# RWKV scan: each head's tokens kept on the half of the partitions that holds its channels, with 64 by 64 products on two quadrants of the array

## Chip, core and metric

The kernel runs on one core of a Trainium2 chip. The metric is the device time of one execution in microseconds (us). PE is the tensor engine (PEld its weight loads), DVE the vector engine, ACT the scalar engine, POOL GpSimd, SP the engine that issues most DMAs.

## What is computed

Two transformer blocks over 512 latent and 256 context tokens of width 1024. The change lies in the second layer of the first block, the RWKV mixer: 16 heads of 64 channels, a state S of 64 by 64 per head, in two directions (forward and backward), first over the context tokens (only the state is kept), then over the latent tokens with output.

```python
def step(s, inp):
    rt, wt, kt, vt, at, bt = inp
    sa = jnp.einsum('bhij,bhj->bhi', s, at)
    s = s * wt[:, :, None, :] + sa[..., None] * bt[:, :, None, :] + vt[..., None] * kt[:, :, None, :]
    y = jnp.einsum('bhij,bhj->bhi', s, rt) if with_out else None
    return s, y
```

The rest of the program (attention, an mLSTM, MLPs, a gated linear attention, experts) is the same before and after.

## The kernel before

The program is written by hand, engine by engine. Every engine runs its instructions in the order of the code, and waits on semaphores for what it needs. PSUM is one ring of eight banks: `K.bank(...)` takes the next one, and waits until whoever read the bank eight takes ago has freed it.

**Projections (`rw_in_*`).** r, v and k are products of the 768 tokens with 1024 by 1024 weights, each split into a rounded part and a rest, so three products each (L770). r and k are made with channels on the partitions (`columns`, 512 and 256 tokens wide), v with tokens on the partitions (`rows`, weights of 256 columns as the moving side, into `a.vR`).

**Scan (`rw_turns`, `rw_pe`, `rw_dve`, `rw_act`, `rw_pool`).** A step of 64 tokens is turned into matrix products. A *unit* is one direction d, one pair of heads m (128 channels: head 0 on partitions 0 to 63, head 1 on 64 to 127), and 256 tokens, that is four chunks of 64. There are 24 units per direction: for each of eight pairs a context unit (b = 0), then two latent ones (b = 1, 2). `rw_turns` lays them out as a pipeline. In iteration n, of twelve turns, both directions *solve* unit n (invert a 64 by 64 triangular matrix per chunk and head), *prepare* unit n+1 (elementwise work), and *stream* unit n-1 (the recurrence, three turns for each chunk). There are three kinds of iteration, which repeat eight times:

- A (n = 0, 3, ...): solves a context unit, streams the last latent unit of the pair before;
- B (n = 1, 4, ...): solves a latent unit, streams a context unit, and holds the norm of the keys of the next pair (`kk`) and the group norm of the outputs of the pair before (`end`);
- C (n = 2, 5, ...): solves a latent unit, streams a latent unit.

**Solve.** Turn 0 makes the gram products (L2355: a with b, and b with a and r); turn 1 the products with k (L2355 again) and four full 128 by 128 transposes of b and k (L2397, L2398), which put tokens on the partitions. Before the change the token chunk j decides on which half of the partitions a product lands, and head hd is in the free dimension, so the gram goes through all four 64 by 64 quadrants of the array. Turns 2 to 5 (squares and X add) and 6 to 9 (blocks of the inverse) are 64 by 64 products on the two diagonal quadrants (L2364, L2418). Between them ACT copies (L2742, L2746) and DVE adds (L2607, L2615, L2622).

**Prepare.** Turn 1 has the low-rank product of a unit (L2377, L2378: 64 rows, 128 columns, 256 tokens; "lora" below), turns 3 to 9 scans, exponentials and multiplications on DVE, ACT and POOL.

**Stream.** For each chunk, part 0 makes `rh` (L2446: a 128-row product with the state `zm`, held as a 128 by 128 matrix with two zero blocks; L2448: two 64 by 64), ACT copies it (L2755), part 1 makes `uu` (L2455), ACT copies it (L2761), part 2 makes `zz` (L2464, four 64 by 64) for the next state, and for latent units the output y (L2470: a 128 by 128 with the state; L2474: four 64 by 64). DVE makes the next state from `zz` (L2639, two instructions, one for each half), with POOL's scaled old state (L2842). At a given chunk the forward direction uses one half of the partitions for tokens, the backward one the other.

A float32 product that is not a transpose stands in the trace as two instructions, so counts there are twice those of the code. A transpose is one.

Of the kernel before, what the change touches and what calls it, by code (L numbers as in the profile page):

```python
# [529 lines left out]
def plan_layer1(K, w_at):  # L530
# [11 lines left out]
    a.vR = hpf[:, 0:6144].rearrange("p (x c) -> p x c", x=6)  # L542
# [21 lines left out]
    for d in range(2):  # L564
# [3 lines left out]
        s.sets = [(K.alloc(2, 4, 64), K.alloc(4, 2, 64), K.alloc(4, 64), K.alloc(2, 2, 128)),  # L568
# [3 lines left out]
                   bk[d].rearrange("p (a i c) -> p a i c", a=2, i=2))]  # L572
        s.RH, s.UU = K.alloc(128), [K.alloc(128) for _ in range(2)]
        z = K.Cf[:, 1600:1984] if d == 0 else K.alloc(384)
        s.zm, s.zg = [z[:, 0:128], z[:, 128:256]], z[:, 256:384]
# [9 lines left out]
    r.sq, r.kavh = K.alloc(768), K.Cf[:, 2024:2032]  # L585
    r.y = K.ring("y", ybufs)
# [1592 lines left out]
def rw_in_pe(K):  # L2179
# [12 lines left out]
    for g in range(12):  # L2192
        what = "rvk"[g // 4]
        lo = a.xx_lo if what == "k" else a.mix_lo
        ready = lambda k: K.at("rw lo", what, k)

        def x(k, x0, x1):
            return a.hi[:, k, x0:x1], lo[:, k, x0 + 1 + x0 // 512 * 2:x1 + 1 + x0 // 512 * 2]

        if what == "v":  # L2200
            through(w.rows(g, "rw v", g - 4, x, ready, wide=g == 4))
        else:
            through(w.columns(g, "rw " + what, 2 * (g % 4), x, BOTH, ready, wide=g % 4 == 0))


def rw_in_act(K):
# [12 lines left out]

    def rows(g):  # L2220
        n = 1 if g == 4 else 2
        for x in range(6 // n):
            s.wait_ge(K.at("rw v", g - 4, x))
            s.e.activation(a.vR[:, n * x:n * x + n, (g - 4) * 256:(g - 3) * 256],
                           K.ps.of("rw v", g - 4, x)[:, 0:n * 256].rearrange("p (x c) -> p x c", x=n), ACT.Copy).then_inc(
                *s.up(free("rw v", g - 4, x)))
# [26 lines left out]
    for g in range(4, 7):  # L2253
        rows(g)
# [3 lines left out]
    rows(7)  # L2258
# [3 lines left out]
    for g in range(8, 12):  # L2262
        columns(g, "rw k", a.kT)
        if g < 10:
            w.act(2 + g)

# [13 lines left out]
class Unit:  # L2280
# [23 lines left out]
    def chunk(self, sub):  # L2304

        it, j = sub // 2, sub % 2 ^ self.d
        return it, j, (*self.key, sub)
# [38 lines left out]
def rw_pe(K):  # L2346
    a, pe = K.a1, K.pe

    def gram(u, out, at, lhs, rhs):

        for it in range(2):
            for j in range(2):
                for hd, o in halves():
                    t = u.toks[it][j]
                    mm = pe.e.matmul(out[hd][half(j), it, at, :], lhs[o, t], rhs[o, :, t], start=True, stop=True)  # L2355
                    if it and j:
                        yield hd, mm

    def blocks(ps, o, lhs, rhs):

        for g in range(4):
            for j in range(2):
                h = half(j)
                mm = pe.e.matmul(ps[h, o + g * 64:o + g * 64 + 64], lhs[h, g, :], rhs[h, g, :], start=True, stop=True)  # L2364
        return mm

    for what, turn, u in rw_turns(K):
        if what == "kk" and turn == 2:
            pe.wait_ge(K.at("kk sq", u))
            for j, (x0, x1) in enumerate(BOTH):  # L2370
                ps = K.bank("norms", u, j)
                pe.e.matmul(ps[:, 0:x1 - x0], K.blk, K.rw.sq[:, x0:x1], start=True, stop=True).then_inc(
                    *pe.up(("norms", u, j)))
        if what == "prep" and turn == 0:
# [5 lines left out]
        if what == "solve":  # L2380
# [3 lines left out]
            if turn == 0:  # L2384
                pe.wait_ge(K.at("made", *u.key))
                out = [K.bank("gram", *u.key, hd)[:, 0:384].rearrange("p (i x c) -> p i x c", i=2, x=3) for hd in range(2)]
                for hd, mm in gram(u, out, slice(1, 2), u.aa, u.ops[:, 1:2, :]):
                    pass
                for hd, mm in gram(u, out, slice(0, 3, 2) if u.lat else slice(0, 1), u.bb, u.ops[:, to, :]):
                    mm.then_inc(*pe.up(("gram", *u.key, hd)))  # L2390
            if turn == 1:
                out = [K.bank("ka", *u.key, hd)[:, 0:256].rearrange("p (i x c) -> p i x c", i=2, x=2) for hd in range(2)]
                for hd, mm in gram(u, out, slice(0, 2 if u.lat else 1), u.ks, u.ops[:, to, :]):
                    mm.then_inc(*pe.up(("ka", *u.key, hd)))
                ps = K.bank("bk", *u.key)
                for it in range(2):
                    pe.e.transpose(ps[:, it * 128:it * 128 + 128], u.bb[:, u.tok[it]], K.ident)  # L2397
# [1635 lines left out]
```

## Time and profile before

| | us |
|---|---|
| median of 3 runs (lowest, highest) | 3886.99 (3884.51, 3895.28) |
| the profiled execution | 3884.07 |
| its span | 3882.3 |

| engine | busy us | share | instructions |
|---|---|---|---|
| PE | 3559.7 | 92% | 31848 |
| PEld | 2596.1 | 67% | 31848 |
| DVE | 1654.1 | 43% | 3457 |
| ACT | 1193.9 | 31% | 2457 |
| POOL | 400.9 | 10% | 608 |

The scan lies at about 1546 to 2445 us of the span. The table is an average over stages with different limits; what an edit is worth is read from its own stage. In a timeline row the first number is the start, the second the time from the first start to the last end of the merged instructions, the last "x" their count, and the bracket the idle time ahead with what ended it. The end of a matmul is later than the start of the next one that follows it at full rate, so rates come from differences between starts, or between ends.

### The profile page before, as it was taken

Reading aid. Unit: us, or ns where it says so; the run is one execution under the profiler, and the core shown is the slowest. Engines: PE = TensorE matmul, PEld = TensorE weight load, DVE = VectorE, ACT = ScalarE, POOL = GpSimd, SP = SyncE. Lnnn points to the kernel's source line nnn. Section 1 sums busy time; section 2 is a strip of 40 time slices with the busy share of each in tenths; the row PEclk is TensorE's granted clock in tenths of the full one; section 3 lists DMA queues with packets and bytes.
Section 4 is the critical chain, followed back from the end, with each engine's and each line's share of the span. In section 5 each row is a group of like instructions: output and inputs, shape, how many; then the busy total and the mean of one; then the engine's idle time right before and its main releaser. Section 6 shows DMA issues by size and latency. Waiting matters only on the chain.

```text
span 3882.3 us, 72541 instructions
## 1 busy us (share of the span) xinstructions
PE 3559.7 (92%) x31848; PEld 2596.1 (67%) x31848; DVE 1654.1 (43%) x3457; ACT 1193.9 (31%) x2457; POOL 400.9 (10%) x608
## 2 busy tenths in 40 slices
PE   7999998999999799799999999799998899698997
PEld 3565567788888498677877777478877677443332
DVE  1253345433333631666666665243343564311112
ACT  2242023412212322454545454232233332200001
POOL 0000122100001000222222222000000300000000
PEclk9999999999999899899999999699999899799998
DMA  5283043211111110000000000222221121489996
GB/s 212 96 338 128 28 163 120 87 65 66 66 66 66 40 66 5 5 4 4 4 4 4 5 4 3 114 88 87 95 79 63 44 92 75 170 366 427 427 428 265
DMA packets 34923, 433.83 MB, mean 112 GB/s; under 512 B 4992, under 2 KB 5600, under 8 KB 9136
## 3 DMA queue, kind: packets, MB, share of 16 engines
q1 hardware_dynamic: 29664, 413.44, 26.7%
q0 software_dynamic: 4944, 15.74, 1.3%
q8 instruction: 252, 4.13, 0.4%
q14 instruction: 63, 0.52, 0.0%
HBM read 423.92 MB, written 5.24 MB: 111 GB/s over the span
## 4 chain that ended last, share of the span: by engine, by line
PE 79%; DMA 9%; DVE 5%; ACT 5%; issue 1%; POOL 1%; SPq 0%; DVEq 0%; ACTq 0%; POOLq 0%
PE ps L770 16%; PE ps L1936 7%; PE ps L1937 7%; PE ps L1938 7%; PE ps L2364 7%; PE ps L711 4%; PE ps L3690 4%; DMA part<-in_wd 4%; DMA part<-in_wg 3%; PE ps L694 3%; PE ps L2446 2%; PE ps L2448 2%; PE ps L1016 2%; PE ps L2470 1%; ACT L71 1%; PE ps L2474 1%
## 5 line engine op out<-in xcount | busy, mean ns | idle before, releaser
L770 PE MATMUL ps<-part 128*128 128x512 f32 (+1 forms) x3312 | 624.0, 351 | 30.5 <-DVE part L1001 11.2
L770 PEld LDWEIGHTS ps<-part 128*128 128x128 f32 x3312 | 532.5, 193 | 122.6 <-DVE part L1001 12.4
L1936 PE MATMUL ps<-part 128*128 128x512 f32 (+1 forms) x1536 | 548.7, 357 | 18.0 <-DVE part L1983 11.4
L1937 PE MATMUL ps<-part 128*128 128x512 f32 (+1 forms) x1536 | 547.9, 357 | 0.0
L1938 PE MATMUL ps<-part 128*128 128x512 f32 (+1 forms) x1536 | 547.6, 357 | 0.0
L3690 PE MATMUL ps<-part 128*64 128x512 f32 x1536 | 377.3, 613 | 38.6 <-DMA part<-in_wd 16.4
L2364 PE MATMUL ps<-part 64*64 64x64 f32 x9984 | 360.9, 221 | 20.8 <-ACT part L2742 10.9
L1960 DVE TENSOR_TENSOR part<-part 128x1024 fp32r<-128x1024 f32 x128 | 158.6, 1239 | 493.6 <-ACT part L1949 493.6
L2364 PEld LDWEIGHTS ps<-part 64*64 64x64 f32 x9984 | 331.7, 135 | 49.7 <-ACT part L2742 17.5
L1936 PEld LDWEIGHTS ps<-part 128*128 128x128 f32 x1536 | 289.7, 189 | 67.8 <-DVE part L1983 12.6
L1937 PEld LDWEIGHTS ps<-part 128*128 128x128 f32 x1536 | 289.7, 189 | 46.4
L1938 PEld LDWEIGHTS ps<-part 128*128 128x128 f32 x1536 | 289.6, 189 | 46.3
L3690 PEld LDWEIGHTS ps<-part 128*64 128x64 f32 x1536 | 126.5, 140 | 270.5 <-issue 188.7
L1949 ACT ACTIVATE part<-part 128x1024 fp32r<-128x1024 f32 x128 | 135.6, 1060 | 485.8 <-PE ps L1938 485.3
L860 POOL TENSOR_TENSOR part<-part 128x512 f32<-128x512 f32 (+1 forms) x48 | 55.8, 1170 | 1765.8 <-ACT part L852 1212.7
L746 DVE TENSOR_TENSOR part<-part 128x2048 fp32r<-128x2048 f32 x40 | 91.4, 2290 | 236.0 <-ACT part L741 235.9
L711 PE MATMUL ps<-part 128*128 128x512 f32 x384 | 172.0, 604 | 2.8 <-ACT part L942 2.4
L711 PEld LDWEIGHTS ps<-part 128*128 128x128 f32 x384 | 73.5, 194 | 91.1 <-issue 88.5
L2639 DVE SCALAR_TENSOR_TENSOR part<-ps,part 64x64 f32<-64x64 f32 x320 | 90.2, 282 | 88.6 <-PE ps L2464 81.2
L694 PE MATMUL ps<-part 128*128 128x256 f32 (+1 forms) x384 | 126.4, 485 | 0.0
L3758 DVE TENSOR_TENSOR part<-part,ps 128x512 f32<-128x512 f32 x32 | 22.0, 688 | 240.1 <-PE ps L3664 113.5
L741 ACT ACTIVATE part<-part 128x2048 fp32r<-128x2048 f32 x44 | 83.8, 1910 | 94.4 <-PE ps L770 70.6
(414 smaller groups left out, 4920.7 us busy)
## 6 DMA issues: line engine op xcount, KB each, us to landing
part<-in_ada_w SPq DMA_DIRECT2D x36, 2048.0 KB, 9.3
part<-in_mlp_w SPq DMA_DIRECT2D x32, 2048.0 KB, 8.0
part<-in_wg SPq DMA_DIRECT2D x32, 2048.0 KB, 22.2
part<-in_wu SPq DMA_DIRECT2D x32, 2048.0 KB, 22.2
part<-in_wd SPq DMA_DIRECT2D x32, 2048.0 KB, 22.2
part<-in_b_in SPq DMA_DIRECT2D x8, 2048.0 KB, 7.9
part<-in_ab_w_in SPq DMA_DIRECT2D x7, 2048.0 KB, 8.7
part<-in_rkv SPq DMA_DIRECT2D x6, 2048.0 KB, 8.1
```

Source lines behind the costliest of these rows:

```text
L694: mm = pe.e.matmul(ps[:, 0:b - a], w[:, k, m:m + 128], h[:, k, a:b], start=k == 0, stop=k == kt - 1)
L711: mm = pe.e.matmul(ps[:, 0:n], h[:, k, o:o + 128], w[:, k, :], start=k == 0, stop=k == kt - 1)
L746: v.e.tensor_tensor(self.rest(g), self.tile(g), self.first(g), SUB).then_inc(*v.up((name, "split", g)))
L770: mm = pe.e.matmul(ps[:, j * n:j * n + n], lhs, rhs, start=k == ks[0] and i == 0, stop=k == ks[-1] and i == 2)
L1936: pe.e.matmul(ps, wh[:, k, :], hi[:, k, x0:x1], start=k == 0, stop=False)
L1937: pe.e.matmul(ps, wh[:, k, :], lo[:, k, x0:x1], start=False, stop=False)
L1938: mm = pe.e.matmul(ps, wl[:, k, :], hi[:, k, x0:x1], start=False, stop=k == 7)
L1949: s.e.activation(b.W[t % 2][0], src, ACT.Copy).then_inc(*s.up(self.key("rounded", t), self.key("split", t), *([("free", "w") + self.key("w ...
L1960: v.e.tensor_tensor(wl, src, wh, SUB).then_inc(*v.up(self.key("split", t), *([("free", "w") + self.key("w", p)] if c == 3 else [])))
L2364: mm = pe.e.matmul(ps[h, o + g * 64:o + g * 64 + 64], lhs[h, g, :], rhs[h, g, :], start=True, stop=True)
L2639: inst = v.e.scalar_tensor_tensor(out=z[o, o], in0=ps, scalar=gain[o], in1=s.zg[o, o], op0=MUL, op1=ADD)
L3690: mm = pe.e.matmul(ps[half(p), :], lhs(k, p), K.panel(8, 512, w, g, c, p)[:, k, :], start=k == 0, stop=k == 7)
```

## The change

- v is projected with channels on the partitions, like r and k (`a.vT`), and turned for each pair of heads in 64 by 64 blocks against the identity (a new helper `turned`, in B at turn 4, two banks), which ACT copies to `r.V` at turn 5 (two instructions). The transposes back at the end (L2494) are gone.
- A head's tokens now lie on the half that its channels lie on. Every product of solve and stream is 64 by 64, head 0 on one diagonal quadrant, head 1 on the other.
- The state is two 64 by 64 blocks above each other (128 partitions, 64 columns), without zero blocks. So the 128-row product in `rh` becomes two 64 by 64, and the 128 by 128 one in y also; DVE makes the next state in one instruction, and POOL scales half the columns.
- The four transposes of b and k become sixteen 64 by 64 products with the identity.
- The gram of turn 0 is only a with b both ways, in one bank. The products with k move from turn 1 to turn 10, that of b with r and the turned b and k to turn 11. Their masks and copies move along (DVE turns 10 and 11, ACT turn 11), and take one instruction where there were two.

```diff
-    def gram(u, out, at, lhs, rhs):
+    def gram(u, out, lhs, rhs):
         for it in range(2):
             for j in range(2):
                 for hd, o in halves():
                     t = u.toks[it][j]
-                    mm = pe.e.matmul(out[hd][half(j), it, at, :], lhs[o, t], rhs[o, :, t], start=True, stop=True)
+                    mm = pe.e.matmul(out[o, 2 * it + j], lhs[o, t], rhs[o, :, t], start=True, stop=True)
...
+    def turned(ps, o, blocks_of):
+
+        for i, block in enumerate(blocks_of):
+            for hd, h in halves():
+                mm = pe.e.matmul(ps[h, o + i * 64:o + i * 64 + 64], block[h, :], K.ident[h, h], start=True, stop=True)
         return mm
...
+        if what == "kk" and turn == 4:
+            for j, (x0, x1) in enumerate(BOTH):
+                ps = K.bank("v turned", u, j)
+                turned(ps, 0, [a.vT[:, u, x:x + 64] for x in range(x0, x1, 64)]).then_inc(*pe.up(("v turned", u, j)))
...
-                    pe.e.matmul(ps[h, 0:128], u.aa[:, cs], zm, start=True, stop=False, skip_group_check=True)
+                    for hd, o in halves():
+                        pe.e.matmul(ps[o, 0:64], u.aa[o, cs], zm[o, :], start=True, stop=False, skip_group_check=True)
...
-                    pe.e.matmul(ps[:, 0:64], zm, u.rr[:, cs], start=True, stop=False, skip_group_check=True)
-                    for k, w in enumerate((uu[h, :], vm)):
+                    sums = (zm, u.rr[:, cs]), (uu, u.Arb[:, g, :]), (vm, u.A[:, g, 1, :])
+                    for k, (w, A) in enumerate(sums):
                         for hd, o in halves():
-                            A = u.A[h, 2 * hd + it, 1, :] if k else u.Arb[h, 2 * hd + it, :]
-                            mm = pe.e.matmul(ps[o, 0:64], w[:, o], A, start=False, stop=k == 1, skip_group_check=True)
+                            mm = pe.e.matmul(ps[o, 0:64], w[o, :], A[o, :], start=k == 0, stop=k == 2, skip_group_check=True)
```

PE, turns 0 and 1 of an iteration that solves a latent unit, before: the two `rh` (L2446, L2448), then for each direction the products with k, four transposes and the low-rank pair.

```order
L2446 MATMUL ps<-part 64x128 [waits dve_wrote]
L2448 MATMUL ps<-part 64x64 x2
L2446 MATMUL ps<-part 64x128 [waits dve_wrote]
L2448 MATMUL ps<-part 64x64 x2
L2355 MATMUL ps<-part 64x128 x8
L2397 MATMUL ps<-part 128x128 [waits dve_wrote,act_wrote]
L2398 MATMUL ps<-part 128x128
L2397 MATMUL ps<-part 128x128
L2398 MATMUL ps<-part 128x128
L2377 MATMUL ps<-part 128x256 [waits landed_po0,landed_po1,dve_wrote,act_wrote]
L2378 MATMUL ps<-part 128x256
```

The same place after: `rh` is L2441 and L2443, the low-rank pair L2376 and L2377, `uu` L2449.

```order
L2441 MATMUL ps<-part 64x64 [waits dve_wrote]
L2441 MATMUL ps<-part 64x64
L2443 MATMUL ps<-part 64x64 x2
L2441 MATMUL ps<-part 64x64 [waits dve_wrote,act_wrote]
L2441 MATMUL ps<-part 64x64
L2443 MATMUL ps<-part 64x64 x2
L2376 MATMUL ps<-part 128x256
L2377 MATMUL ps<-part 128x256
L2376 MATMUL ps<-part 128x256 [waits act_wrote]
L2377 MATMUL ps<-part 128x256
L2449 MATMUL ps<-part 64x64 [waits act_wrote]
```

Nothing of 128 rows is left in `rh`, and the low-rank products of the two directions now stand side by side.

ACT, turns 4 to 6 of a B iteration, after: L2667 and L2669 are the key norm, L2724 the copies of squares, L2744 `uu`, L2758 the squares of y, L2675 the new copies of v, L2694 an exponential of the preparation.

```order
L71 ACT_TABLE_LOAD [waits dve_wrote]
L2667 ACTIVATE part<-part 128x768
L2669 ACTIVATE part<-part 128x768 [waits act_wrote]
L2724 ACTIVATE part<-ps 128x256 [waits pe_wrote] x2
L2744 ACTIVATE part<-ps 128x64 [waits pe_wrote] x2
L2758 ACTIVATE part<-part 128x512
L2675 ACTIVATE part<-ps 128x512
L2675 ACTIVATE part<-ps 128x256
L71 ACT_TABLE_LOAD [waits dve_wrote]
L2694 ACTIVATE part<-part 128x256
```

Before, the same stretch has no row between the squares of y (L2776) and the table load:

```order
L2742 ACTIVATE part<-ps 128x256 [waits pe_wrote] x2
L2761 ACTIVATE part<-ps 64x128 [waits pe_wrote] x2
L2776 ACTIVATE part<-part 128x512
L71 ACT_TABLE_LOAD [waits dve_wrote]
L2710 ACTIVATE part<-part 128x256
```

The two copies of v are the only thing that ACT has more there, and they are what frees the two banks that the turned v took.

## Rows read from the trace of the kernel before

**Rows 1.** Busy time by stretch: one A, one B, one C iteration.

```profile
core 0: us, PE busy (x) PEld busy (x) DVE busy (x) ACT busy (x) POOL busy (x), PEclk, DMA share, GB/s
1985.60:2018.30 32.70, 32.26 (x775) 27.66 (x775) 20.59 (x60) 15.96 (x50) 8.83 (x17) 1.00 0.01 4
2018.30:2058.90 40.60, 34.82 (x726) 27.14 (x728) 27.20 (x73) 23.58 (x54) 11.37 (x22) 0.96 0.02 6
2058.90:2093.10 34.20, 33.42 (x792) 28.36 (x784) 23.33 (x72) 14.79 (x47) 7.31 (x15) 1.00 0.01 4
```

**Rows 2.** The chain that ended last, a piece of an A iteration.

```profile
1996.17 2.80 PE ps L2364 x93
```

**Rows 3.** Timeline of PE in A: turn 9, both directions' part 0.

```profile
2006.64 0.63 PE L2364 MATMUL ps<-part 64*64 64x64 f32 x15
2007.20 0.43 PE L2446 MATMUL ps<-part 128*64 128x128 f32 x2
...
2007.93 0.43 PE L2446 MATMUL ps<-part 128*64 128x128 f32 x2
...
2008.52 0.22 PE L2448 MATMUL ps<-part 64*64 64x64 f32 x1
```

**Rows 4.** Timeline of PE in A: a latent part 2, both directions.

```profile
1994.16 0.28 PE L2364 MATMUL ps<-part 64*64 64x64 f32 x3
...
1994.59 0.43 PE L2470 MATMUL ps<-part 128*128 128x64 f32 x2
...
1995.94 0.23 PE L2474 MATMUL ps<-part 64*64 64x64 f32 x2
```

**Rows 5.** Timeline of PE: the gram of an A iteration, then of a B.

```profile
1985.70 1.10 PE L2355 MATMUL ps<-part 64*64 64x64 f32 x62
...
2018.40 1.51 PE L2355 MATMUL ps<-part 64*64 64x64 f32 x62
```

**Rows 6.** Timeline of PE in A, turn 1: transposes and lora of one direction.

```profile
1988.11 0.40 PE L2355 MATMUL ps<-part 64*64 64x64 f32 x7
...
1989.02 0.70 PE L2377 MATMUL ps<-part 64*128 64x256 f32 x2
...
1990.08 0.46 PE L2355 MATMUL ps<-part 64*64 64x64 f32 x16
```

**Rows 7.** Timeline of PE at the scan's start: both directions' lora together.

```profile
1558.73 1.23 PE L2377 MATMUL ps<-part 64*128 64x256 f32 x4
```

**Rows 8.** Timeline of PE in B: waits at turns 5 and 8.

```profile
2039.09 0.97 PE L2364 MATMUL ps<-part 64*64 64x64 f32 x26 [1.56 <-ACT part L2742]
...
2051.45 0.74 PE L2464 MATMUL ps<-part 64*64 64x64 f32 x16 [2.78 <-ACT part L2761]
```

**Rows 9.** Timeline of ACT in the same B.

```profile
2040.44 1.28 ACT L71 ACT_TABLE_LOAD   x1
...
2045.87 1.28 ACT L71 ACT_TABLE_LOAD   x1 [1.50 <-DVE part L2660]
```

**Rows 10.** Groups by line over the scan: DVE's state update, ACT's 512-wide copy.

```profile
L2639 DVE SCALAR_TENSOR_TENSOR part<-ps,part 64x64 f32<-64x64 f32 x306 | 86.2, 282 | 75.7 <-PE ps L2464 68.6 <-POOL part L2842 0.4
...
L2736 ACT ACTIVATE part<-ps 128x512 f32<-128x512 f32 x47 | 28.1, 599 | 5.5 <-PE ps L2398 4.0
```

**Rows 11.** Busy time of DVE, turns 3 to 9 of an A.

```profile
1995.70:2016.20 20.50, 15.89 (x46) 1.00 0.01 3
```

**Rows 12.** Busy time by stretch, just after the wait at turn 8.

```profile
2053.40:2056.60 3.20, 3.20 (x40) 2.57 (x37) 2.67 (x6) 0.84 (x2) 0.92 (x1) 0.50 0.00 0
```

**Rows 13.** Timeline of PE in the tail: two successive chunks.

```profile
2410.68 0.43 PE L2446 MATMUL ps<-part 128*64 128x128 f32 x2
...
2414.77 0.43 PE L2446 MATMUL ps<-part 128*64 128x128 f32 x2
```

**Rows 14.** Busy time of PE on L770: projection of r, then of v.

```profile
1333.10:1401.00 67.90, 67.81 (x384) 58.99 (x384) 1.00 0.09 31
1404.30:1474.10 69.80, 69.69 (x576) 69.67 (x576) 0.98 0.14 53
```

More of the change, by code:

```diff
@@ L2198, in x @@
             return a.hi[:, k, x0:x1], lo[:, k, x0 + 1 + x0 // 512 * 2:x1 + 1 + x0 // 512 * 2]
[L2200 to L2203, printed above, removed]
+        through(w.columns(g, "rw " + what, 2 * (g % 4), x, BOTH, ready, wide=g % 4 == 0))
 def rw_in_act(K):
@@ L2253, in rw_in_act @@
     for g in range(4, 7):
-        rows(g)
+        columns(g, "rw v", a.vT)
         w.act(2 + g)
@@ L2257, in rw_in_act @@
     first(a.xx, 0, "k")
-    rows(7)
+    columns(7, "rw v", a.vT)
     for k in range(1, 8):
@@ L2414, in rw_pe @@
                 pe.wait_ge(K.at("X", *u.key, 3))
-                for g in range(4):
-                    for j in range(2):
-                        h = half(j)
-                        mm = pe.e.matmul(ps[h, g * 64:g * 64 + 64], XX[h, 0, g, :], K.ident[h, h], start=True, stop=True)
-                mm.then_inc(*pe.up(("X turned", *u.key)))
+                turned(ps, 0, [XX[:, 0, g, :] for g in range(4)]).then_inc(*pe.up(("X turned", *u.key)))
             if turn in (6, 8):
@@ L2490, in rw_pe @@
                 pe.e.matmul(ps, K.blk, k0, start=True, stop=True).then_inc(*pe.up(("coef", m)))
-            if turn == 5:
-                ps = K.bank("v turned", m)
-                for x in range(4):
-                    mm = pe.e.transpose(ps[:, x * 128:x * 128 + 128], a.vR[:, x, m * 128:m * 128 + 128], K.ident)
-                mm.then_inc(*pe.up(("v turned", m)))
 def rw_dve(K):
@@ L2692, in rw_act @@
                 s.e.activation(r.sq, r.sq, ACT.Exp, scale=-0.5, bias=float(7 * np.log(2.0))).then_inc(*s.up(("kk rstd", m)))
+            if turn == 5:
+                if m >= 2:
+                    s.wait_ge(*[K.at("streamed", d, 3 * m - 4) for d in range(2)])
+                for j, (x0, x1) in enumerate(BOTH):
+                    s.wait_ge(K.at("v turned", m, j))
+                    s.e.activation(r.V[m % 2].rearrange("p x c -> p (x c)")[:, x0:x1], K.ps.of("v turned", m, j)[:, 0:x1 - x0],
+                                   ACT.Copy).then_inc(*s.up(("v rows", m), free("v turned", m, j)))
         if what == "prep":
@@ L2726, in rw_act @@
                     s.wait_ge(K.at(("PX", 2), u.d, u.n - 1))
[L2727 to L2732 removed]
+                s.wait_ge(K.at("gram", *u.key), K.at("masked", *u.key))
+                src = K.ps.of("gram", *u.key).rearrange("p (g x c) -> p g x c", g=4, x=2)
+                s.e.activation(t.Pf, src[:, :, 1, :], ACT.Copy).then_inc(*s.up(("Pf", *u.key), free("gram", *u.key)))
+            if turn == 11:
                 s.wait_ge(K.at("bk", *u.key))
```

171 lines of the change are left out of this document (72 added, 99 removed).

## The prediction, as put on record

> **What bounds the kernel now.** I read the busy time by stretch first [rows 1]. In all three kinds of iteration PE is the fullest engine: 32.26 of 32.7 us in A, 33.42 of 34.2 in C, at full clock, with DVE at 63 to 68% and ACT at 43 to 49%. In B it is different: PE 34.82 of 40.6, ACT 23.58, and two waits of PE of 1.56 and 2.78 us on ACT [rows 8]. So A and C are worth what PE is spared, as long as DVE keeps up, and B is worth what the chain through ACT is spared. A group of three takes 107.5 us, eight groups 860 us.
>
> Then the rate of small products. A stretch of L2364 has 93 instructions in 2.80 us, 0.030 each [rows 2]: two per 0.06 us, one on each diagonal quadrant. The gram, which goes through all four, has 62 in 1.10 us [rows 5], with 0.22 of that the last one's own length 0.0144 each: twice the rate. And a change of shape costs: two `rh` last from the end of L2364 (2006.64 + 0.63) to the end of the last L2448 (2008.52 + 0.22), 1.47 us for twelve instructions [rows 3].
>
> **The change, part by part.** Times are for both directions; all float32 products count as two instructions.
>
> *Part 0 (`rh`).* Eight products of one shape, 16 x 0.030 = 0.48, for 1.47: -0.99. A has four, C four, B three (the first context chunk has no state).
>
> *Part 2.* For a latent chunk 1.73 us from 1994.16 + 0.28 to 1995.94 + 0.23 [rows 4]. After, twenty products, 40 x 0.030 = 1.20: -0.53. The last chunk of a pair has no `zz`: about 1.45 before (1.73 less eight instructions), 24 x 0.030 = 0.72 after: -0.7. For a context chunk the two directions today can use four quadrants; 16 instructions cost 0.23 to 0.48 before and 0.48 after; I take +0.15 each, +0.6 in B.
>
> *Part 1* stays at eight instructions on two quadrants: nothing.
>
> *Gram.* It leaves four quadrants for two. A: 64 instructions, 0.92 to 1.92: +1.0. B and C: today 1.51 less 0.22, 1.3 us, in which half of the instructions are 128 columns wide; after 64 narrow ones, 1.92: +0.6.
>
> *Products with k.* A: 32 narrow ones, 0.46 to 0.96: +0.5. B and C: wide ones; from the B gram, (1.3 - 0.47) / 32 = 0.026 each on four quadrants, so 0.83 to 1.66: +0.83. *b with r* is new by itself in B and C: 32 x 0.030 = +0.96.
>
> *Transposes and lora.* For one direction from the last start of L2355 (1988.11 + 0.40 - 0.22) to its next at 1990.08 [rows 6], less one slot 1.75 us, so 3.5 for two. After, the turned blocks are 64 x 0.030 = 1.92 us. The two lora products now stand together. At the scan's start they already do, and four instructions take 1.23 us at half clock [rows 7], where two alone take 0.70 at full clock [rows 6]: they run side by side. So 1.06 (1989.02 to 1990.08) plus 0.2 for the change of shape, 1.26, and together 3.2: -0.3. If they ran one after the other, +0.7.
>
> *v.* B gets 48 x 0.030 = 1.44 us of turned v and loses four transposes with their changes of shape, at most 0.73 (1988.29 to 1989.02 in rows 6): +0.75. ACT gets a copy of 512 columns, 0.60 [rows 10], and one of 256, about 0.4.
>
> PE alone: A +1.0 +0.5 -0.3 -4.0 -1.6 -0.7 = -5.1. C +0.6 +0.83 +0.96 -0.3 -4.0 -2.1 = -4.0. B +0.6 +0.83 +0.96 -0.3 -3.0 +0.6 +0.75 = +0.4.
>
> *What comes through.* In A and C the cover is DVE. In turns 3 to 9 of A it is busy 15.89 of 20.5 us [rows 11]. The state update goes from four instructions of 0.282 [rows 10] to two for each chunk, -1.1 in these turns, so 14.8. PE's share of these turns goes from 20.5 to about 16.5 (three `rh`, two parts 2). DVE is then 90% full there and hands its results to PE in a chain, and I add 0.4 us of waits to A and 0.3 to C: -4.7 and -3.7. The moved products lie in turns 10 and 11, ahead of `uu` and `zz`, where they cover the copies of `rh` and `uu` on ACT.
>
> In B turns 0 to 3 lose 3.3 us on PE (gram +0.6, k -0.83, transposes and lora 3.5 to 1.26, one `rh` -1.0, `zz` +0.15), so ACT's chain of table loads and exponentials [rows 9] starts that much earlier. It gets 1.0 us of copies of v, which stand ahead of its second table load. They also free the two banks of the turned v. Six more banks are taken in turn 4, so the ring of eight comes round to the first of these two at the first X add of turn 5: **PE waits there for the copies**, some 2.9 us instead of 1.56. The wait at turn 8 is set by the same chain and is released 2.1 us earlier than today. Behind it PE has more to do: +1.66 +0.96 +1.92 -1.0 -0.7 +0.3, less 0.5 us of a wait that is now covered, +2.7. B comes out at +0.6.
>
> The clock belongs in this. After the wait at turn 8 the granted clock is 0.50 for 3.2 us (1.2 GHz) [rows 12], which costs 1.6 us in each B; it was 1.00 before. That stays in my sum. The trace has the slow clock behind a gap of 2.78 us, and the new wait at turn 5 is of that size. The Trainium skill (TensorE: Matmul & The Clock Gate, Why this matters for your kernels) advises against long idle gaps between bursts of matmuls, since idling brings the slow clock back; the trace agrees at turn 8, and the same thing at turn 5 is the second rival below.
>
> *Sum.* Seven A with a stream, 7 x -4.7 = -32.9; the first, with nothing to stream, +1.2; eight C, -29.6; eight B, +4.8. In the tail a chunk takes 4.1 us [rows 13], where PE, ACT and DVE take turns; PE is spared 1.5 us a chunk, four chunks, -6. The projection of v as columns costs what r costs, 67.9 for 69.8 [rows 14]: -1.9. At the scan's start ACT's copies add about 1. Together -63. From the profiled execution's 3884.1 that is 3821; the median of the runs lies 2.9 above that execution, so the forecast is 3824.
>
> **Rivals.**
>
> *DVE, and the chains through it, take half of what A and C gain.* Turns 3 to 9 shrink by 2 us instead of 4. For it: 90% of a chained engine; POOL's large multiplications slow DVE beside them. Against it: today these chains let PE wait under 1 us an iteration. Fifteen times +2: 3854.
>
> *A second spell of slow clock in B.* The wait at turn 5 grows to the size of the one at turn 8, and 1.7 us are lost behind it in seven B: 3836.
>
> *The lora products do not overlap at full clock.* +1.0 in 23 iterations: 3847.
>
> *Better.* The waits of A and C (0.4 and 0.8 us by rows 1) vanish with DVE's shorter updates, and B gains from its earlier chain: -27, 3797.
>
> *Slower: two quadrants for four, with nothing gained for it.* The added work (gram, k, b with r: 1.5 + 2.4 + 2.4, v 0.75, context 0.6, less 0.9 of lora) is 6.8 us in a group, the spared 15.3 (11 x 0.99, 7 x 0.53, 0.7). If what is spared is filled by waits, the kernel gets slower once less than 44% of it comes through; with none, 8 x 6.8 = +54 on today's 3887, 3941. That needs DVE to grow in turns 3 to 9 instead of shrinking, or a wait of 4 us in every A and C.
>
> *The two halves of a product share a bank, and exclude each other.* Every new product would then cost 0.060 an instruction instead of 0.030; some 1200 instructions in a group, +36 us, eight times: 4112. Against it: L2364 already writes both halves of one bank, at 0.030 [rows 2]. The Trainium skill (TensorEngine Tiling (Array Packing), Gotcha 1: PSUM Pressure) says that different row tiles cannot access the same PSUM bank at the same time; the trace of this kernel does not agree where the halves of the partitions differ.
>
> **How the numbers follow.** Forecast as summed 0.42; DVE takes half 0.18; slow clock 0.15; lora 0.07; better 0.12; slower 0.04; bank 0.02. The range from 3790 to 3858 takes in all but the last two and some spread around the others. A measurement of this kernel tells about 0.3%, 12 us, from no change. Faster by more than that holds all but 0.07; I split the rest into 0.03 within and 0.04 slower.
>
> **What would show it.** Part 0 of both directions in 0.5 us and part 2 in 1.2; the gram of A in 1.9; A near 28 us, C near 30.5, B near 41; DVE busy over 85% in turns 3 to 9; in B a wait of nearly 3 us before the X add of turn 5, released by ACT's copy of v, and the wait at turn 8 still there; L770 of v at 68 us. I am wrong if A and C keep more than 31 and 33 us with PE waiting for DVE, or if B grows by more than 3 us.

## The result, and the profile of the changed kernel

The changed kernel takes 3775.9 us (median of four runs, 3767.3 to 3785.3), the kernel before, timed beside it, 3889.8 (four runs, 3884.5 to 3895.3): a ratio of 0.971, 95% interval 0.968 to 0.974. That is 114 us less, where the forecast had 65; the time lies 14 us below the lower end of the range. Of the runs below, one execution of the split state update took 5785.6 us at a granted clock of 0.55 and is left out of its median.

The profiled execution is the slowest of the four, 3785.3 us. It comes to the stages ahead of the projections about 10 us later than the one of before, though nothing is changed there, so that the pair of traces differs by 99 us only. Its page:

```profile
span 3783.5 us, 77347 instructions
PE 3472.2 (92%) x34472; PEld 2594.7 (69%) x34472; DVE 1595.7 (42%) x3149; ACT 1152.0 (30%) x2426; POOL 387.6 (10%) x608
```

The three kinds of iteration, from gram to gram, answer [rows 1]; the fourth stretch, PE's turns 3 to 9 of A, answers [rows 11], and the fifth, behind the wait at turn 8 of B, [rows 12]:

```profile
core 0: us, PE busy (x) PEld busy (x) DVE busy (x) ACT busy (x) POOL busy (x), PEclk, DMA share, GB/s
1952.43:1978.93 26.50, 26.35 (x862) 25.70 (x860) 18.67 (x50) 13.38 (x47) 8.52 (x17) 1.00 0.02 5
1978.93:2019.07 40.14, 34.31 (x864) 29.45 (x862) 26.11 (x63) 22.41 (x56) 10.94 (x22) 0.96 0.03 7
2019.07:2047.78 28.71, 28.56 (x910) 27.91 (x908) 19.20 (x54) 13.22 (x46) 6.29 (x15) 1.00 0.02 4
1959.25:1975.20 15.95, 15.80 (x534) 15.58 (x532) 13.45 (x39) 7.24 (x28) 6.77 (x14) 1.00 0.02 5
2011.20:2014.40 3.20, 3.20 (x61) 3.16 (x62) 1.98 (x5) 1.04 (x3) 0.10 (x1) 0.60 0.00 0
```

A went from 32.7 to 26.5 us, C from 34.2 to 28.7, B from 40.6 to 40.1. In A and C, PE is now idle for 0.15 us. DVE's busy time in A fell by 1.9 us, ACT's by 2.6. PE's timeline over the start of an A (here line 2345 is the gram, 2441 and 2443 are `rh`, 2376 and 2377 lora, 2449 `uu`) answers [rows 3, 5, 6]:

```profile
1952.43 2.03 PE L2345 MATMUL ps<-part 64*64 64x64 f32 x64
1954.30 0.28 PE L2441 MATMUL ps<-part 64*64 64x64 f32 x4
1954.42 0.28 PE L2443 MATMUL ps<-part 64*64 64x64 f32 x4
1954.53 0.28 PE L2441 MATMUL ps<-part 64*64 64x64 f32 x4
1954.65 0.28 PE L2443 MATMUL ps<-part 64*64 64x64 f32 x4
1954.86 0.71 PE L2376 MATMUL ps<-part 64*128 64x256 f32 x4
1955.40 0.60 PE L2377 MATMUL ps<-part 64*128 64x256 f32 x4
1955.93 0.45 PE L2449 MATMUL ps<-part 64*64 64x64 f32 x8
```

The gram takes 1.87 us from start to start, part 0 of both directions 0.56 (0.47 where narrow products follow, at 1962.05 to 1962.52), and both lora 1.07 together, x4 and x4 where [rows 6] has x2 and x2 for one direction.

**Where the time went, term by term.** I charged each PE instruction of one group (A, B and C, gram to gram) with the time from its start to the start of the next; what is left of a gap behind the instruction's own length is a wait. So a change of shape is charged to somebody. In us a group:

| | before | after | difference | forecast |
|---|---|---|---|---|
| `rh` and `uu` | 19.31 | 9.37 | -9.9 | -10.9 |
| `zz` and `y` | 14.72 | 10.98 | -3.7 | -3.8 |
| gram, products with k, b with r | 7.60 | 11.90 | +4.3 | +6.3 |
| lora, transposes, turned blocks | 13.39 | 13.08 | -0.3 | -0.15 |
| L2364, now L2352 | 40.92 | 38.81 | -2.1 | 0 |
| norms and sums of the end (slow clock in one) | 4.67 | 5.08 | +0.4 | 0 |
| waits | 6.95 | 6.13 | -0.8 | +0.9 |
| group | 107.5 | 95.35 | -12.2 | -7.7 |

Four and a half us a group are 36 us in eight; the first and the last iterations, which are not quite like this group, bring that to 40 (from the first gram to the tail 96.5 us were saved, where the forecast had 56.5). The rest of what was missed, 9 us, is in the tail.

### The profile page after: what moved, and what is told of

Read it like the earlier page. It is cut to its first block, busy times and chain, and to the rows that moved or that the text cites. A ratio compares the mean times of both kernels' runs of the same rounds, so it can differ in the third digit from the quotient of the medians.

```text
span 3783.5 us, 77347 instructions
## 1 busy us (share of the span) xinstructions
PE 3472.2 (92%) x34472; PEld 2594.7 (69%) x34472; DVE 1595.7 (42%) x3149; ACT 1152.0 (30%) x2426; POOL 387.6 (10%) x608
## 4 chain that ended last, share of the span: by engine, by line
PE 78%; DMA 9%; DVE 6%; ACT 5%; issue 1%; POOL 1%; SPq 0%; DVEq 0%; ACTq 0%; POOLq 0%
PE ps L770 16%; PE ps L1936 8%; PE ps L1938 8%; PE ps L1937 8%; PE ps L2352 7%; PE ps L3672 5%; PE ps L711 4%; DMA part<-in_wd 4%; DMA part<-in_wg 3%; PE ps L694 3%; PE ps L2345 3%; PE ps L1016 2%; PE ps L2359 2%; PE ps L2467 1%; ACT L71 1%; PE ps L2458 1%
## 5 line engine op out<-in xcount | busy, mean ns | idle before, releaser
L770 PE MATMUL ps<-part 128*128 128x512 f32 (+1 forms) x3120 | 627.1, 363 | 30.7 <-DVE part L1001 11.0
L770 PEld LDWEIGHTS ps<-part 128*128 128x128 f32 x3120 | 525.7, 194 | 132.5 <-DVE part L1001 12.2
L2352 PE MATMUL ps<-part 64*64 64x64 f32 x9984 | 343.7, 220 | 20.7 <-ACT part L2675 11.9
L2352 PEld LDWEIGHTS ps<-part 64*64 64x64 f32 x9984 | 318.2, 136 | 48.8 <-ACT part L2675 12.8
L2345 PE MATMUL ps<-part 64*64 64x64 f32 (+1 forms) x2816 | 110.2, 230 | 11.2 <-DVE part L2552 11.2
L741 ACT ACTIVATE part<-part 128x2048 fp32r<-128x2048 f32 x44 | 83.7, 1910 | 95.1 <-PE ps L770 71.7
```

The lines of the kernel that those rows point to most:

```text
L770: mm = pe.e.matmul(ps[:, j * n:j * n + n], lhs, rhs, start=k == ks[0] and i == 0, stop=k == ks[-1] and i == 2)
L2345: mm = pe.e.matmul(out[o, 2 * it + j], lhs[o, t], rhs[o, :, t], start=True, stop=True)
```

## The experiments

Runs of different kernels are compared through their ratios to before, whose intervals are 0.13% to 0.2% to either side (0.3% for the changed kernel); the lengths of iterations in the traces are finer. Here they run from one lora product to the next (the start of turn 1), so they differ a little from those above. A and C are the usual values, B is the mean of six.

| | C | A | B | group | median us | ratio to before |
|---|---|---|---|---|---|---|
| before | 33.2 | 32.25 | 42.2 | 107.7 | 3889.8 | 1 |
| changed | 28.7 | 26.3 | 40.1 | 95.1 | 3775.9 | 0.971 |
| e1_wide | 32.8 | 30.3 | 43.7 | 106.8 | 3865.9 | 0.9935 |
| e2_narrow | 29.65 | 27.2 | 40.1 | 97.0 | 3794.8 | 0.975 |
| e3_copies | 28.8 | 26.3 | 41.0 | 96.1 | 3778.8 | 0.971 |
| e4_state | 29.8 | 26.9 | 41.4 | 98.1 | 3797.1 | 0.977 |
| e5_early | 29.8 | 29.1 | 40.8 | 99.6 | 3812.6 | 0.980 |
| e6_late_v | 31.1 | 26.3 | 39.8 | 97.2 | 3788.5 | 0.973 |
| e7_fill | 28.7 | 26.3 | 38.8 | 93.8 | 3770.1 | 0.969 |
| e9_apart | 30.0 | 27.6 | 40.8 | 98.4 | 3805.3 | 0.979 |
| e10_order | 28.7 | 26.3 | 37.6 | 92.6 | 3757.4 | 0.967 |
| e11_orders | 28.7 | 26.3 | 42.2 | 97.2 | 3790.3 | 0.975 |
| e12_best | 30.1 | 26.3 | 39.4 | 95.7 | 3778.5 | 0.973 |

**A wide product back in part 0.**

```diff
                     pe.wait_ge(K.at("zm", *c))
+                pe.e.matmul(ps[0:64, 128:256], u.aa[:, cs], K.ident, start=True, stop=True)
```

> The changed kernel with one product of 128 rows by 128 columns more at the head of every part 0, into columns of the bank that nobody reads: the shape change of before is back, with all else as changed. Theory (PE's own time sets A and C, and what the change bought there is shapes that no longer change): before, part 0 of one direction took 1.47 / 2 = 0.735 us, of which four narrow instructions at 0.030 are 0.12, so the wide pair with its changes of shape costs 0.6; eight of these in an iteration, 4.9 us, 24 iterations, 117, less what B's waits take up: +95 to +125 us on the changed kernel's 3776, which eats all of its gain. Rival (PE has room, and the gain came from ACT's and DVE's smaller tiles): less than +50. Tail: the granted clock of the last chunks goes back to 0.50 if the wide products are what it goes with.

Measured: +90 us, A +4.1, C +4.1, B +3.6. Divided by eight, a wide product among narrow ones costs 0.51 us, a little under the 0.6 expected, and so the total is just under the range expected. PE's timeline of two part 0 in this run (line 2440 is the added product):

```profile
1995.40 2.97 PE L2352 MATMUL ps<-part 64*64 64x64 f32 x96
1998.30 0.43 PE L2440 MATMUL ps<-part 128*64 128x128 f32 x2
1998.66 0.33 PE L2443 MATMUL ps<-part 64*64 64x64 f32 x4
1998.83 0.28 PE L2445 MATMUL ps<-part 64*64 64x64 f32 x4
1999.04 0.43 PE L2440 MATMUL ps<-part 128*64 128x128 f32 x2
```

From the wide one's start to the next start are 0.36 us, for two instructions. And 2443 and 2445 hold PE for 0.38 us, where without the wide ones they take 0.23: the change is paid on both sides. So the shapes are the main thing that the change bought; the run keeps the narrow products that took the wide one's place, 0.12 us each time, so it gives back somewhat more than part 0 had gained. The tail's clock stayed at 1.00: the wide products alone are not what its 0.50 goes with.

**The control: two narrow products instead.**

```diff
+                for hd, o in halves():
+                    pe.e.matmul(ps[o, 128:192], u.aa[o, cs], K.ident[o, o], start=True, stop=True)
```

> The control: the changed kernel with a 64 by 64 product on each diagonal quadrant more at the head of every part 0 (four instructions where the run with a wide product has two). No change of shape. Theory: four instructions at 0.029 are 0.12, eight times an iteration 0.94, all of it in A and C, less than half in B: +15 to +22 us. Rival (PE has room): under +5. If it costs as much as the wide one, the cost is not the shape but another link in the chain of a chunk.

Measured: +19 us, A and C +0.94 each, just the four instructions eight times. B stayed at 40.1. Twice as many instructions as the wide product at a quarter of its price: it is the shape, and A and C have no room for PE work.

**ACT's copies in two halves.**

```diff
+                for o in (slice(0, 32), slice(32, 64)):
+                    s.e.activation(t.RH[:, o], K.ps.of("rh", *c)[:, o], ACT.Copy)...   (and UU alike)
```

> The changed kernel with each of ACT's copies of rh and uu made as two copies of half the columns: about +0.2 us in the chain for each copy, four times what they got shorter by (0.27 to 0.225). Theory (A and C bound by PE): A and C get under 0.3 us more each, B, which waits for ACT, 1 to 1.5: +10 to +18 us in all. Rival (the waits that went, 0.3 in A and in C, went because of the shorter copies, and the chain of a chunk is close to setting the end): waits of 0.2 us at most of the eight chunks of A and C, +1 us or more each, +25 us or more.

Measured: +3 us, less than the +10 to +18 expected; A and C grow by under 0.1 in most of their iterations, B by 0.9. The rival falls. That ACT's copies got shorter did not take the waits of A and C away.

**DVE's state update in two halves.**

```diff
-                    inst = v.e.scalar_tensor_tensor(out=z, in0=ps, scalar=gain, in1=s.zg, op0=MUL, op1=ADD)
+                    for hd, o in halves():
+                        inst = v.e.scalar_tensor_tensor(out=z[o], in0=ps[o], scalar=gain[o], in1=s.zg[o], ...)
```

> The changed kernel with DVE's state update again as two instructions of 64 partitions, as before: +0.28 us on DVE for each chunk and direction. DVE is busy 13.45 of 15.95 us in turns 3 to 9 of A. Theory (PE sets A and C, DVE has room): under +0.2 us an iteration, +0 to +6 us. Rival (what I had not counted is that DVE's shorter updates took the waits of A and C away): the waits of 0.3 us come back and more, +0.5 us or more in A and C, +8 to +20 us.

Measured: +21 us (median of three runs; +24 by the ratios), C +1.1, A +0.6, B +1.3. Here the rival held, at the upper end of its range or above it. Six of this run's seven A take 26.9 us and have a wait of PE ahead of the second `rh` of turn 6 (first row) and one of 0.12. The second row is DVE at that place:

```profile
1874.58 0.33 PE L2441 MATMUL ps<-part 64*64 64x64 f32 x4 [0.25 <-ACT part L2742]
1873.21 1.22 DVE L2616 SCALAR_TENSOR_TENSOR part<-ps,part 64x64 f32<-64x64 f32 x4
...
1980.31 0.33 PE L2441 MATMUL ps<-part 64*64 64x64 f32 x4 [0.18 <-DVE part L2616]
```

Line 2616 is the state update, four instructions for the two directions, and the last ends at 1874.43, 0.15 us before PE goes on. (The copy that the first row names ends at 1874.59, after `rh` has started, so it was not what PE waited for.) In the seventh A, of 27.5 us, the profile names the update itself (last row). PE stands at `rh` until the state is there. One instruction of 128 partitions costs DVE what one of 64 cost, in the group over the scan:

```profile
L2615 DVE SCALAR_TENSOR_TENSOR part<-ps,part 128x64 f32<-128x64 f32 x160 | 40.5, 278 | 63.8 <-PE ps L2458 63.5
```

0.278 us for 0.282 twice [rows 10]. So of the 114 us some 21 to 24 rest on DVE's half of the change, and it is what keeps the waits away that I had put into the sum. A and C have 13 of them; of B's 1.3 a part is that the clock was slow for longer in three of its six B (42.3 us each, where two others took 41.1).

**The moved products back in turn 1.**

```diff
-            if turn == 10:
+            if turn == 1:          (k; and 11 to 1 for b with r and the turned blocks; on DVE and ACT alike)
```

> The changed kernel with the products with k, b with r and the turned b and k back in turn 1, where before had them; PE's products are the same ones. Theory (where they stand matters): in A and C they cover ACT's copies of rh and uu in turns 10 and 11, 0.3 to 0.6 us an iteration; in B they come ahead of ACT's chain and no longer behind it: +1 to +2 us. In all +12 to +30 us. Rival (PE is full in A and C wherever they stand, and B's chain has room): within 5 us of the changed kernel.

Measured: +37 us, A +2.8, C +1.1, B +0.7. The theory's total is passed, but not by its mechanism. By the same charging as above, lora goes from 3.28 us a group to 6.35, which is 3.1 of this group's 4.5 us: the moved products again stand between the two directions' lora. `uu` adds 0.9, for the copies are no longer covered. B did not get what was expected there.

**Lora apart.**

```diff
+            if u.d:
+                for hd, o in halves():
+                    pe.e.matmul(ps[o, 0:64], K.ident[o, o], K.ident[o, o], start=True, stop=True)
             pe.e.matmul(ps[:, 0:256], u.wm[u.rows, 0, :], a.wh[u.rows, u.lo:u.hi], start=True, stop=True)
```

> The changed kernel with one 64 by 64 product on each diagonal quadrant (four instructions, result overwritten) between the lora products of the two directions, which stand next to each other there. With the products moved back to turn 1 lora cost 6.35 us a group instead of 3.28. Theory (the two directions' lora run side by side, each on its half of the rows, only when they stand together, and that is what the moved products bought): +1.0 us for lora and 0.1 for the four instructions in each of 24 iterations, +22 to +28 us. Rival (it was the place of the moved products themselves): +3 us.

Measured: +29 us, C and A +1.3, B +0.7. PE's timeline with the four narrow instructions (line 2378) between:

```profile
1988.56 0.70 PE L2379 MATMUL ps<-part 64*128 64x256 f32 x2
1989.10 0.59 PE L2380 MATMUL ps<-part 64*128 64x256 f32 x2
1989.62 0.33 PE L2378 MATMUL ps<-part 64*64 64x64 f32 x4
1989.88 0.70 PE L2379 MATMUL ps<-part 64*128 64x256 f32 x2
1990.41 0.59 PE L2380 MATMUL ps<-part 64*128 64x256 f32 x2
```

Each direction takes 1.06 us again, one after the other, against 1.07 for both above. Four instructions between them undo the overlap. This settles the move: most of what it is worth is that lora stands together. The four are of another shape than lora; that instructions of the same shape between them would do the same was not tried.

**The turned v out of B.**

```diff
-        if what == "kk" and turn == 4:
+        if what == "v" and turn == 6:      (in the next iteration; ACT's copies in its turn 7)
```

> The changed kernel with the turned v and ACT's copies of it in the iteration after B (turns 6 and 7) instead of turns 4 and 5 of B. Theory (the 1.77 us wait at turn 5 of B is made by these copies): the wait goes, and B gets 1.4 us shorter by the products besides, less what the wait at turn 8 grows by; the other iteration gets 1.4 us longer, PE being full there. Net -0.5 to -1.5 us a group, -4 to -12 us. Rival (the chain of ACT's table loads sets B, and the wait at turn 8 takes over what the one at turn 5 gives): B shorter by no more than the products, 0 to +5 us.

Measured: +13 us, outside both ranges. B shrinks by 0.3 only, the other iteration grows by 2.4, of which 0.8 is a wait for this copy. In B the wait at turn 5 is still there, with another releaser, and the one at turn 8 a little longer:

```profile
1995.91 1.15 PE L2354 MATMUL ps<-part 64*64 64x64 f32 x32 [1.66 <-ACT part L2728]
...
2007.45 1.12 PE L2460 MATMUL ps<-part 64*64 64x64 f32 x16 [2.98 <-ACT part L2748]
```

L2728 is ACT's copy of the squares. In the changed kernel that wait names the copy of v (below), but taking it out gives 0.1 us: behind ACT's table load all its copies are late alike.

**Work in the gap at turn 8.**

```diff
+                if sub == 2 and u.b == 0 and u.d == 0:
+                    for i in range(16):
+                        for hd, o in halves():
+                            pe.e.matmul(ps[o, 256:320], u.aa[o, cs], K.ident[o, o], start=True, stop=True)
                 pe.wait_ge(K.at("uu in", *c), K.at("BK", *u.key))
```

> The changed kernel with 64 narrow instructions, 1.87 us, whose result nobody reads, ahead of the wait of 2.66 us at turn 8 of B. Theory (the granted clock of 0.60 in the 3.2 us behind that wait is due to the gap): the clock stays at 1.00 there and the wait is 0.8 us: 1.0 to 1.3 us less in each B, -8 to -10 us. Rival (the clock falls with something else, or the products delay what comes behind): 0 to +5 us.

The waits of B in the changed kernel, then what this run has at the same two places, then two stretches of this run, around the second wait and behind it:

```profile
1997.95 1.15 PE L2352 MATMUL ps<-part 64*64 64x64 f32 x32 [1.77 <-ACT part L2675]
...
2009.16 0.68 PE L2458 MATMUL ps<-part 64*64 64x64 f32 x16 [2.66 <-ACT part L2744]
```

```profile
1985.18 1.15 PE L2352 MATMUL ps<-part 64*64 64x64 f32 x32 [1.77 <-ACT part L2680]
...
1996.39 0.68 PE L2463 MATMUL ps<-part 64*64 64x64 f32 x16 [0.79 <-ACT part L2749]
```

```profile
1994.90:1998.40 3.50, 2.71 (x53) 1.75 (x51) 2.70 (x6) 1.55 (x6) 2.46 (x4) 1.00 0.02 5
1998.40:2001.00 2.60, 2.60 (x72) 2.60 (x70) 2.41 (x6) 1.05 (x3) 0.13 (x1) 1.00 0.03 6
```

The granted clock stays at 1.00, where it was 0.60, and every B is 38.8 us, 1.5 less than most in the changed kernel (40.4). By the runs -6 us, a little under what was expected, which alone the intervals do not tell from nothing. Work that nobody needs made the kernel no slower.

The gap does not bring the slow clock each time. In the changed kernel itself five B have the 2.66 us and the slow clock; the last two have as long a wait (2.66 and 2.60) and keep 1.00, and the first of these takes 38.8 us:

```profile
2199.86 0.68 PE L2458 MATMUL ps<-part 64*64 64x64 f32 x16 [2.66 <-ACT part L2744]
...
2201.90:2205.10 3.20, 3.20 (x90) 3.20 (x86) 2.83 (x7) 1.09 (x4) 0.10 (x1) 1.00 0.01 3
```

In the control with two narrow products, where that wait is 2.59 us, three of six B had the slow clock, in this run none of six.

**Work in the gaps of before's tail.**

```diff
                 ps = K.bank("uu", *c)
+                if u.n == UNITS - 1:
+                    for hd, o in halves():
+                        for i in range(2):
+                            pe.e.matmul(ps[o, 256:320], u.aa[o, cs], K.ident[o, o], start=True, stop=True)
                 pe.wait_ge(K.at("rh in", *c), K.at("X", *u.key, 5))
```

> The kernel before, with eight narrow instructions more (0.23 us, their result read by nobody) ahead of each wait for the copy of rh in the last iteration alone, for both directions. There its granted clock is 0.50 from 2415 to the end of the scan, a chunk takes 6.3 us, and the changed kernel has 1.00 and 2.6 us a chunk. Theory (short gaps bring the slow clock): the clock stays at 1.00 in the last chunks, -6 to -12 us on before. Rival (it is not the gaps): the clock falls as before, +1 to +3 us.

The tail by stretch, first the kernel before, then the changed one, then this run:

```profile
2411.00:2416.40 5.40, 5.11 (x66) 3.73 (x64) 1.13 (x4) 1.83 (x8) 0.99 (x3) 0.88 0.00 0
2416.40:2422.70 6.30, 5.95 (x58) 4.40 (x58) 1.13 (x4) 1.53 (x6) 0.80 (x2) 0.50 0.00 0
2422.70:2429.00 6.30, 5.95 (x57) 4.40 (x56) 1.13 (x4) 1.54 (x6) 0.00 (x0) 0.50 0.01 3
```

```profile
2325.00:2327.60 2.60, 2.60 (x72) 2.21 (x70) 0.57 (x3) 1.34 (x6) 0.58 (x2) 1.00 0.02 6
```

```profile
2416.00:2420.00 4.00, 3.93 (x72) 3.11 (x71) 0.91 (x4) 1.32 (x6) 0.49 (x3) 1.00 0.00 0
2420.00:2424.00 4.00, 4.00 (x73) 3.25 (x73) 1.14 (x4) 1.53 (x6) 0.73 (x2) 1.00 0.01 4
```

Measured: 3884.1 for 3893.3 beside it, ratio 0.998, interval 0.996 to 0.999, -9 us. Sixty-four added instructions bring the full clock back to the last chunks. Before, that clock fell with PE busy 5.11 of 5.4 us. From the first `rh` of the tail to the start of the last product of the scan before took 31.4 us, in this run 24.4, in the changed kernel 16.5. So of the -14.9 about 7 is this clock, a little over 6 the shorter chunks that the forecast had, and 1.5 the last products, where the transposes of v are gone. Each of these is one profiled execution; the ten of this run give -9 us with an interval of -4 to -14.

**ACT's order in turn 7 of B.** The turns list yields, for ACT alone and in this turn of B, the solve and the stream ahead of the preparation.

```diff
-    for what, turn, u in rw_turns(K):
+    for what, turn, u in rw_turns(K, (7,)):
```

> The changed kernel with ACT's order changed in turn 7 of B alone: its copies of uu come ahead of the four exponentials of the next unit and their table load, not behind them. The copies take 0.34 us; behind them PE waits 2.66 us at turn 8, and then has the slow clock. Theory (that wait is the place of two copies in ACT's queue, not the load of ACT): the wait falls under 0.5 us and the clock stays at 1.00: 2.5 to 3.5 us less in each B, -18 to -26 us. Rival (ACT's whole chain sets B, so that the wait turns up later, at the gram or at turn 9): 0 to -6 us.

Measured: 3757.4 us (3754.5 to 3759.5), ratio 0.967, interval 0.965 to 0.968. Every B is 37.6 us, 2.8 less than most in the changed kernel. The wait of 2.66 at turn 8 is gone; of what it held back, 1.04 shows up two steps later, released by DVE, with the clock at 1.00. This is at the lower end of what the theory expected. It is the fastest version here, 132 us under before (3757.4 for 3889.8) and 18 under the changed kernel.

```profile
1990.49 0.68 PE L2368 MATMUL ps<-part 64*64 64x64 f32 x16 [0.16 <-DVE part L2619]
...
1994.58 0.68 PE L2368 MATMUL ps<-part 64*64 64x64 f32 x16 [1.04 <-DVE part L2612]
```

**The same in turns 4 and 5.**

```diff
+    for what, turn, u in rw_turns(K, (4, 5, 7)):
```

> As the run with ACT's order changed in turn 7, and in turns 4 and 5 of B too: the copies of the solve and of the stream come ahead of the logarithm, the exponential and their table load, and ahead of the copies of v. Theory (the wait of 1.77 us at turn 5, too, is the place of a copy in the queue): 1.0 to 1.7 us less in each B than with turn 7 alone, -26 to -38 us on the changed kernel. Rival (the later logarithm makes kk late, and the next unit's operands with it): between the changed kernel and the run with turn 7 alone.

Measured: 3790.3, 33 us worse than turn 7 alone and 14 above the changed kernel: neither the theory nor the rival had it so slow. ACT now waits 1.97 us for the squares of turn 4, and only then come the table load, the logarithm and the exponential, and the copies of v (L2691) behind them; PE waits for those at turn 5:

```profile
1994.38 0.38 ACT L2740 ACTIVATE part<-ps 128x256 f32<-128x256 f32 x1 [1.97 <-PE ps L2368]
...
1999.38 0.85 ACT L2691 ACTIVATE part<-ps 128x512 f32<-128x512 f32 x2
```

```profile
2000.01 1.98 PE L2368 MATMUL ps<-part 64*64 64x64 f32 x32 [4.51 <-ACT part L2691]
```

**Turns 4 and 7, with v out of B.**

```diff
+    for what, turn, u in rw_turns(K, (4, 7)):
...
-        if what == "kk" and turn == 4:
+        if what == "v":                     (turn 10 of the iteration after B)
```

> A version meant to be faster. From the run with turn 7's order (3757), two more edits: the turned v and ACT's copies of it in turn 10 of the iteration before the one with k's products in A, out of B (in turns 6 and 7 of that iteration they cost 2.4 us, of which 0.8 is a wait for the copy), and in turn 4 of B ACT's copies of the solve come ahead of the logarithm and its table load. Theory (with the v copies gone, the wait at turn 5 is the place of a copy in ACT's queue behind the table load): B loses 1.4 us of products and up to 1.7 of the wait, the other iteration gains 1.4 to 1.6: -1.0 to -1.7 us a group, 3744 to 3750, 0.964 of before. Rival (the later logarithm sets B, as in the run where all the orders changed): 3757 or more.

Measured: 3778.5 (five runs), 21 us worse than turn 7 alone. The rival held. The logarithm that now starts later makes DVE's `kk` late, and that multiplication (L2525, on DVE) stands ahead of the X addition (L2606) that PE waits for:

```profile
1996.76 0.96 DVE L2525 TENSOR_TENSOR part<-part 128x768 f32<-128x768 f32 x1 [2.27 <-ACT part L2687]
```

```profile
1998.23 1.12 PE L2377 MATMUL ps<-part 64*64 64x64 f32 x16 [3.37 <-DVE part L2606]
```

## Why the prediction was wrong: the steps one by one

**What bounds the kernel** was read rightly: PE in A and C (the control's products came through in full), ACT's chain in B.

**Part 0.** Forecast -10.9 a group, measured -9.9. The size of -0.99 was close; part 0 of two directions takes 0.56 instead of 0.48, in starts. The experiment with the wide product shows this step's mechanism by itself. The Trainium skill (TensorEngine Tiling (Array Packing), Tiling Modes) says that a change of tiling mode drains TensorE; the 0.51 us for a wide product among narrow ones, against 0.12 for two narrow ones, agrees.

**Part 2, lora and the turned blocks** came out as summed: -3.7 for -3.8, and -0.3 for -0.15. That the lora products run side by side at full clock, which I read from the scan's start at half clock [rows 7], is confirmed, and the rival in which they do not is what the lora-apart run built.

**Gram and products with k: mis-sized by 2.0 us a group.** I took the best rate in the trace, 62 instructions in 1.10 us [rows 5], for all of them. It holds for the gram alone. The products with k stood elsewhere, on PE's timeline of before:

```profile
1987.47 0.43 PE L2446 MATMUL ps<-part 128*64 128x128 f32 x2
1987.83 0.27 PE L2448 MATMUL ps<-part 64*64 64x64 f32 x1
1987.84 0.28 PE L2355 MATMUL ps<-part 64*64 64x64 f32 x3
...
1988.11 0.40 PE L2355 MATMUL ps<-part 64*64 64x64 f32 x7
1988.44 0.33 PE L2397 MATMUL ps<-part 128*128 128x128 f32 x1
```

They run between `rh` and the transposes, with a change of shape at the end; charged from start to start, A's 96 instructions held PE 1.98 us. I had counted 1.38 (0.92 and 0.46). Two quadrants instead of four cost them much less than double.

**The blocks: 2.1 us a group that I had not seen at all.** I counted L2364 as untouched, and inside a stretch it is: 0.030 an instruction before and after. But its 1248 instructions held PE 40.9 us before and 38.8 after. Much of the difference stands at the borders, where a stretch's last instruction is followed by another shape or another pair of quadrants. In nine places of a group it is followed by `rh`: there it held PE 0.16 us on average before, ahead of a wide product, and 0.05 after. That is 1.0 of the 2.1 us, and it fits the run with the wide product back, where these instructions hold PE 0.3 us longer in each A and C. The other 1.1 is spread over the other borders and the stretches themselves; how much of it belongs to the shape and how much to the pair of quadrants is open, for no run separates them.

**Waits: forecast +0.9 a group, measured -0.8.** I expected DVE at 90% of turns 3 to 9 and a chain that holds PE up. In PE's 15.95 us of these turns DVE is busy 13.45, 84%, but its own work of turn 9 ends 1.37 us later:

```profile
1959.25:1976.57 17.32, 14.78 (x41) 1.00 0.02 4
```

So DVE's load came out as forecast, 14.8 us, 1.1 less than before, and PE still waited for it 0.15 us an A. The step that failed is that I weighed DVE by its busy share and not by its place: the merged update shortens the link from `zz` to the next `rh`, and the run that splits it again gives 0.6 to 1.1 us to A and C.

**B.** Forecast +0.6, measured -0.5. At turn 5 the wait was released by ACT's copy of v, as forecast, and was 1.77 us for 2.9; that name was no cause, as the run without those copies in B showed. The wait at turn 8 stayed (2.66 for 2.78), with the slow clock behind it (0.60 for 3.2 us). The run with turn 7 reordered shows that it was no matter of ACT's load: two copies of 0.16 us stood behind a table load and four exponentials.

**The tail: -6 forecast, -14.9 measured.** I took the step between two chunks at full clock [rows 13] for all four. The ones behind them had a granted clock of 0.50 and took 6.3 us each. That was in the trace of before, unread: 7 of the 9 us. The other 2 are mostly the transposes of v at the end of the scan, which I had left out.

**Projection of v.** Forecast -1.9; it took 70.2 us against 69.8, with the clock at 0.96 where r's took 67.9 at 1.00 before and after [rows 14]. The slow start that v's had before stayed.

```profile
1414.30:1484.50 70.20, 70.14 (x384) 60.95 (x384) 0.96 0.13 51
```

**The rivals.** DVE taking half, a second slow spell at turn 5, lora in sequence, two quadrants exclusive in a bank and slower: none came. "Better", at 0.12, was nearest, in its signs (no waits in A and C), with half of the size (its -27 stands without its working); and the narrow pairs, which share a bank, kept to 0.029 an instruction.

Summed: of the 49 us between forecast and result, borders are 17, the k products 16, waits 14, the tail 9; part 0 (-8), and the clock at one sum product (-3) go against it; the 4 that are left lie in the first and the last iterations. The mechanism was right, products of one shape where PE bounds; the sum failed in four terms, two of which, the borders and the tail's clock, it put at nothing.

## What to carry to other kernels

Charge each instruction of the engine that bounds with the time to the next start, over a whole period, and work from these sums. Lengths of well-formed stretches leave out what changes of shape cost the neighbours; here borders and a rate taken from the best stretch made 33 of 114 us. When products of two directions use different halves of the array, put them next to each other with nothing between. Read an in-order engine's wait by its place in the queue: moving two short copies ahead of a table load gave 18 us, more than the filler in front of the same wait, while moving others in the same way took back 33.

## What the runs showed of the chip

- One fp32 product of 128 rows among 64 by 64 ones costs 0.51 us, its own 0.36 to the next start included; a pair of 64 by 64 ones 0.12.
- Products of 64 rows by 256 columns on the two halves of the rows take 1.07 us for both when they stand together, and 1.06 each with four narrow instructions between.
- The granted clock fell to 0.50 (1.2 GHz) in a tail where PE was busy 95% of the time and its waits were 0.3 us, stayed there to the end of the chunks, and did not fall with 0.23 us of added products ahead of each wait. The changed kernel's tail, with as short chunks and small gaps, and the one with wide products put back, kept 1.00. What of these makes the difference is open.
- A DVE instruction of 128 partitions by 64 takes 0.278 us, one of 64 by 64 takes 0.282; ACT's copy of 128 by 64 takes 0.224, and of 64 by 128, 0.270. In these four the time goes with the elements in a partition, not with the number of partitions.
- A wait of PE of 2.66 us brought the granted clock to 0.50 behind it in five B of the changed kernel, worth 1.5 us each, and did not in two. A wait of 0.8 us at that place, behind added products, did in none of six.
